# Two attentions of a three-layer block on one core: where factors, rests and gatings stand in the vector engine's order

## The reference

```
o1 = sweep_attention(qq[..., 0, :], kk[..., 0, :], vv)
o2 = sweep_attention(qq[..., 1, :], kk[..., 1, :], vv)
o = o1 - lam.astype(o1.dtype) * o2
o = rms_norm(o, subln_g) * (1.0 - lam_init)
return (o * jax.nn.silu(gate)) @ w_out
```

## Time and profile before

| | |
|---|---|
| median of three runs | 805.94 us |
| profiled execution, its own time | 805.69 us |
| its span | 803.7 us |
| PE busy | 789.2 us, 98% |
| DVE busy | 505.1 us, 63% |
| ACT busy | 393.8 us, 49% |
| granted PE clock | 1.00 |

### The profile page before, as it was taken

One profiled execution on the slowest core, in us unless ns is written; L12 is line 12 of the kernel. 1 busy time (PEld: TensorE's weight loads), 2 busy tenths in 40 slices (PEclk: granted clock), 3 DMA queues, 4 the chain that ended last, 5 costly groups with the idle time before them and its releaser, 6 DMA issues. The chain is left out here.

```text
span 803.7 us, 11013 instructions
## 1 busy us (share of the span) xinstructions
PE 789.2 (98%) x4108; PEld 626.2 (78%) x4108; DVE 505.1 (63%) x873; ACT 393.8 (49%) x728; POOL 42.9 (5%) x55
## 2 busy tenths in 40 slices
PE   9999999999999999999999999999999999999998
PEld 5577787777777778777778877887788888888886
DVE  3474545225768776669856667799887645556454
ACT  3541323235878673575636646735245533343431
POOL 0120000000001001002100001300000000000000
PEclk9999999999999999999999999999999999999999
DMA  9974552355000037337432016883216655466521
GB/s 338 388 239 153 210 192 80 147 210 200 11 1 1 1 119 275 105 105 274 172 105 75 31 64 211 300 308 125 79 53 210 208 180 187 158 201 214 176 91 52
DMA packets 71303, 125.56 MB, mean 156 GB/s; under 512 B 2714, under 2 KB 28652, under 8 KB 71124
## 3 DMA queue, kind: packets, MB, share of 16 engines
q1 hardware_dynamic: 70208, 122.47, 43.8%
q0 software_dynamic: 512, 1.18, 0.5%
q10 hardware_dynamic: 532, 1.21, 0.5%
HBM read 123.79 MB, written 1.06 MB: 155 GB/s over the span
## 5 line engine op out<-in xcount | busy, mean ns | idle before, releaser
L822 PE MATMUL psum<-w_hi,act_hi 128*128 128x512 f32 (+1 forms) x712 | 289.6, 407 | 3.0 <-DVE w_lo L1973 1.0
L823 PE MATMUL psum<-w_lo,act_hi 128*128 128x512 f32 (+1 forms) x752 | 291.9, 388 | 0.0
L824 PE MATMUL psum<-w_hi,act_lo 128*128 128x512 f32 (+1 forms) x712 | 276.8, 389 | 0.0
L1948 DVE TENSOR_TENSOR w_lo<-raw,w_hi 128x2048 fp32r<-128x2048 f32 (+1 forms) x70 | 157.9, 2262 | 103.5 <-ACT w_hi L1369 103.4
L1369 ACT ACTIVATE w_hi<-raw 128x2048 fp32r<-128x2048 f32 (+1 forms) x74 | 139.9, 1895 | 71.2 <-PE psum L824 36.6
L822 PEld LDWEIGHTS psum<-w_hi,act_hi 128*128 128x128 f32 x712 | 133.7, 188 | 45.8 <-issue 17.3
L823 PEld LDWEIGHTS psum<-w_lo,act_hi 128*128 128x128 f32 x752 | 141.6, 188 | 25.4 <-issue 1.0
L824 PEld LDWEIGHTS psum<-w_hi,act_lo 128*128 128x128 f32 x712 | 133.7, 188 | 28.6
L1916 POOL TENSOR_TENSOR rstd<-ms,half_neg 128x1 f32<-128x1 f32 (+3 forms) x38 | 36.3, 957 | 557.6 <-DVE ms L1989 557.6
L1526 ACT ACTIVATE sc<-psum,nmax 128x512 f32<-128x512 f32 (+1 forms) x64 | 36.7, 585 | 24.2 <-DVE nmax L2196 24.2
L1451 ACT ACTIVATE sc<-psum 128x512 f32<-128x512 f32 (+1 forms) x62 | 32.4, 525 | 16.2 <-PE psum L925 8.7
(11 more groups left out here) (272 smaller groups left out, 991.1 us busy)
## 6 DMA issues: line engine op xcount, KB each, us to landing
raw<-in_a_w_in SPq DMA_DIRECT2D x16, 1024.0 KB, 9.8
raw<-in_ada_w SPq DMA_DIRECT2D x16, 1024.0 KB, 5.3
raw<-in_w_out SPq DMA_DIRECT2D x12, 1024.0 KB, 5.1
raw<-in_w_gate SPq DMA_DIRECT2D x22, 512.0 KB, 4.1
raw<-in_w_up SPq DMA_DIRECT2D x22, 512.0 KB, 5.2
raw<-in_w_down SPq DMA_DIRECT2D x11, 1024.0 KB, 5.0
raw<-in_b_w_in SPq DMA_DIRECT2D x10, 1024.0 KB, 7.7
raw<-in_w_in SPq DMA_DIRECT2D x10, 1024.0 KB, 5.9
```

The lines of the kernel that those rows point to most:

```text
L822: pe.matmul(oh, x_hi, hi, start=(k == 0), stop=False)
L823: pe.matmul(o[:, 0:n], x_hi, lo, start=False, stop=False)
L824: mm = pe.matmul(oh, x_lo, hi, start=False, stop=(k == KT - 1))
L1948: ins = dve.tensor_tensor(rest, weights, hi.bitcast(F32), ALU.subtract)
```

## The change

Five edits, all in DVE's program but for one index in ACT's.

- `rinv` has four places instead of two, in `comb0` and `out0` by p % 4; the reciprocal of p waits for the copy of p-4.
- In steps 26 and 28 of the first attention, `to_feature` (rests of the turned tile) stands ahead of `beside0` (the z gating).
- In the second attention the z gatings of steps 3 and 7 move to 4 and 8 and stand behind the half piece of rests; those of 11 and 15 stay in their steps, also behind the half piece. Half pieces move from steps 4, 5, 6, 8 to 5, 6, 7, 9.
- The first output gating (`gated1(0, 0, 4)`) moves from step 9 to step 11, behind the z gating.
- After the loop the last half piece of rests stands ahead of the last output and its gating.

```diff
-RESTS_BESIDE1 = {4: 0, 5: 1, 6: 0, 8: 1, 10: 0, 13: 1, 15: 0}
+RESTS_BESIDE1 = {5: 0, 6: 1, 7: 0, 9: 1, 10: 0, 13: 1, 15: 0}
+GATED_BESIDE1 = {4: (3, 0), 8: (3, 1), 11: (4, 0), 15: (4, 1)}
...
-        rinv = sb("rinv", [P, 2, 4])
+        rinv = sb("rinv", [P, 4, 4])
...
-                r = rinv[:, p % 2, 0:1]
+                r = rinv[:, p % 4, 0:1]
...
-                r = rinv[:, p % 2, :]
-                if p >= 2:
-                    dve.wait_ge(*moved(("pv0", p - 2)))
+                r = rinv[:, p % 4, :]
+                if p >= 4:
+                    dve.wait_ge(*moved(("pv0", p - 4)))
...
                 if p % 2 == 0:
                     comb0(p)
+                if p in (26, 28):
+                    to_feature("turn_o0", [0], parts=((p - 26) // 2,))
                 beside0(p - 1)
...
-                if p in (26, 28):
-                    to_feature("turn_o0", [0], parts=((p - 26) // 2,))
...
-                if p % 4 == 3:
-                    c, t = z_units1[p // 4]
-                    gate_z(zbuf[:, t, (c - 3) * COLS:(c - 2) * COLS], ("in1", c, t))
                 if p in RESTS_BESIDE1:
                     split_piece(RESTS_BESIDE1[p])
-                if p == 9:
+                if p in GATED_BESIDE1:
+                    c, t = GATED_BESIDE1[p]
+                    gate_z(zbuf[:, t, (c - 3) * COLS:(c - 2) * COLS], ("in1", c, t))
+                if p == 11:
                     gated1(0, 0, HEADS // 2, s_v)
...
+            split_piece(1)
             out1(XT * HEADS - 1)
             gated1(1, HEADS // 2, HEADS, s_tok)
-            split_piece(1)
```

More of the change, by code:

```diff
@@ L2467, in gated1 @@
                                                    op0=ALU.mult, op1=ALU.mult).then_inc(done, 1), done)
-            z_units1 = [(c, t) for c in (3, 4) for t in range(XT)]
             dve.wait_ge(*seq.last)
```

## The result

| | before | after |
|---|---|---|
| median of four runs each, same chip | 805.93 us (805.83 to 806.41) | 799.48 us (798.99 to 799.71) |
| ratio | | 0.9918 [0.9901, 0.9935] |
| profiled execution, its own time | 805.69 us | 799.71 us |
| its span | 803.7 us | 797.6 us |

The forecast was 799.8 (798.8 to 802.2), and 6.1 us off the profiled execution, whose span lost 6.1. So the total came out. Lines of the changed kernel up to the reciprocal of the second attention are those of before plus three; after it, plus two.

A forecast was written before the change was run, and what follows sets the result against it. The tensor engine's queue was taken to bound both attentions. Terms: 4.7 (first attention) + 0.8 - 0.6 + 1.2 = 6.1 us off the profiled 805.69, giving 799.6, against the median 799.8; range 798.8 to 802.2.

The forecast's parts named there:

- What bounds the kernel: Both attentions: the tensor engine's queue sets the end; by starts it loses 5.0 us in the first, by idle time 3.00.
- Rival A: Both attentions: only visible idle comes back, 3.00 us in the first; 3.9 in all, so 802.0 us; chance 0.08.
- Four places: First attention, softmax factors: the combination no longer waits for the copy of p-2; gain 3.9 us, from 0 to 4.2.
- The floor of a pair: First attention: a heavy and a light step without loss, from one heavy transpose to the next, taken as 6.65 us.
- Rests ahead of the gating: First attention, step 28: the weight block no longer waits for the turned tile's rests; gain 0.8 us, or none if late.
- Gatings a step on: Second attention, gatings of steps 3 and 7 a step later: stall of 0.77 us goes, 0.1 at step 7; gain 0.8.
- Weight rests a step on: Second attention, four half pieces moved a step later: they run in the vector engine's waits for scores; cost 0.
- Output gating to step 11: Second attention: a second instruction ahead of step 13's maximum delays the values of step 12; cost 0.6 us, at most 1.2.
- The last rest: After the second attention's loop: rests ahead of the last output let the second weight half start on time; gain 1.2 us.
- B: First attention: a second release close behind the removed one holds half of the combinations; 801.8 us; chance 0.06.
- C: Behind the first attention: its gain is given back where x and the next weights are fetched; 804.5 us; chance 0.03.
- D: Second attention: the vector queue becomes the bound, 0.77 us a step in eleven steps; slower, 808.5 us; chance 0.03.

## Why the prediction was right, step by step

- **What bounds the kernel.** Right. The vector stalls counted only where they reached PE, and reading starts instead of idle time decided the size: 3.00 us of idle time, 5.53 regained. Rival A would have had 3.0.
- **Four places: the mechanism right, the term too small**, 3.9 for 4.95. Two errors of one sign. The floor of a pair, 6.65, still held 0.03 to 0.04 of waiting, over fifteen pairs 0.5. And I took off 0.3 for the uncertainty of that floor, though a floor read from one pair can only be too high. Beyond that, about 0.2 of the 0.8 that I had given to the rests was this part's: with four places they are worth 0.58 by starts. 3.9 + 0.5 + 0.3 + 0.2 is the 4.95, but for rounding. The bound "4.2 from above" was no bound.
- **Rests ahead of the gating: too large alone**, 0.8 for 0.28, and 0.6 on top of the four places. I had asked what is late next at the weight block and not at the values a step later. The errors of the two parts overlap; together they brought 5.53 for 4.7.
- **Step 30: not foreseen.** 0.32 given back. I went through the heavy steps for the vector engine alone; this stall is the scalar queue's.
- **Gatings a step on:** 0.8 for 0.85. **Weight rests a step on:** no stall behind steps 5, 6, 7, 9, cost 0.
- **Output gating to step 11:** 0.6 for 0.60, at the place and by the chain named (the 0.05 by which the copy must be ahead is read from the earlier trace rows, not the earlier trace rows). Putting it back showed it.
- **The last rest:** 1.2 for 1.18, or 1.31 with the longer spacing of the block behind the wait, a term that I had counted for the values and not here. And I had credited one edit. I had mentioned that the piece of step 15 would fill the wait for the tanh, and not that this alone does nearly all of it.
- **The start of the span:** 0.62 later in the profiled execution. It hid 0.6 of a sum that otherwise comes to 6.7; the medians differ by 6.45. So the sum was 0.6 too small, and an unrelated 0.6 made the profiled spans agree with it: luck, in size and sign.
- **Rivals.** B fell: no second release held the combinations; the pairs are level. C fell: to the second attention 5.18 of 5.21 are kept. D fell: no stall in steps 5 to 11, and none in 13 to 15.

## What to carry to other kernels

Read what a stall costs from start to start. A smallest distance of many is no floor if every one of them waits: here all fifteen pairs did, and the smallest is the 6.65 that I took. Put the floor together from the smallest of each part (3.11 + 3.48), and look at whether the record of the instructions at its ends is the short one (0.60) or the long one (0.66). When a writer waits for a reader that stands in another engine's queue, one more place is enough if only the newest reader is late; look then at the scalar and the tensor queue for who is late next, step by step to the loop's end, where the filler work thins out. Optional work belongs in a queue's waits, and never between a release and a reduction whose consumer has a quarter of a microsecond in hand.

## What the runs showed of the hardware

Four transposes that start the moment their data arrive take 0.66 us in the record, those whose data are there 0.60, with the same four instructions. A values product is written as 1.16 after a wait and 1.05 without. I had counted this start-up for the values (0.11 in steps 4 and 12) and not for the transposes, where it makes up the part of the floor that I missed. That the cause is a weight load which the wait leaves uncovered is my reading; no run isolates it.
